# A gated MLP rewritten in two phases: up-projection by two levels of Strassen with weight sums made by accumulating DMAs, down-projection with resident weights

## What is computed

```python
hn = rmsnorm(x, norm1_g);  proj = hn @ w_in            # 1024 -> 3608
# ... both head groups, chunked; mix = concat(o_a, o_b)
x = x + mix @ w_out
hn2 = rmsnorm(x, norm2_g)
up, ffn_new = causal_dwconv(hn2 @ w_up, st_ffn, ffn_conv_w)   # 1024 -> 2*2816, float32
a_f, b_f = jnp.split(up, [D_FF], axis=-1)              # D_FF = 2816 = 22 * 128
x = x + (jax.nn.silu(a_f) * b_f) @ w_down              # 2816 -> 1024
y = rmsnorm(x, norm_f_g)
```

## Time and profile before

| | |
|---|---|
| median of 3 runs | 3259.01 us (3258.15 to 3260.91) |
| profiled execution, span from first to last instruction | 3255.5 us |
| mixers, to the first matmul of the MLP | 1600.7 us |
| MLP, from there to the end of the span | 1654.8 us |
| PE busy | 3173.5 us, 97% of the span |
| DVE busy | 2029.6 us, 62% |
| ACT, POOL busy | 26%, 18% |

### The profile page before, as it was taken

One profiled execution on the slowest core, in us unless ns is written; L12 is line 12 of the kernel. 1 busy time (PEld: TensorE's weight loads), 2 busy tenths in 40 slices (PEclk: granted clock), 3 DMA queues, 4 the chain that ended last, 5 costly groups with the idle time before them and its releaser, 6 DMA issues.

```text
span 3255.5 us, 56610 instructions
## 1 busy us (share of the span) xinstructions
PE 3173.5 (97%) x22353; PEld 2088.1 (64%) x22353; DVE 2029.6 (62%) x4672; ACT 833.7 (26%) x1743; POOL 580.7 (18%) x935
## 2 busy tenths in 40 slices
PE   7999999999999999997799999999999999999998
PEld 4555565566655565554577777777767767777765
DVE  2556666655566665655565666666676666666668
ACT  2222333223223333233321112111232211221213
POOL 1111111111111110112331211121053121111110
PEclk9999999999999999997899999999999999999999
DMA  7022222222222222215611111111133111111112
GB/s 242 27 67 85 85 77 75 85 67 69 66 75 85 85 66 85 80 52 159 205 50 39 52 52 39 39 52 39 39 124 119 48 43 52 39 39 39 47 31 78
DMA packets 223188, 236.37 MB, mean 73 GB/s; under 512 B 14204, under 2 KB 167332, under 8 KB 222931
## 3 DMA queue, kind: packets, MB, share of 16 engines
q1 hardware_dynamic: 222931, 232.81, 22.7%
HBM read 203.10 MB, written 29.67 MB: 72 GB/s over the span
## 4 chain that ended last, share of the span: by engine, by line
PE 50%; DVE 1%; issue 0%; ACT 0%; DVEq 0%
PE mlp_bank L2139 33%; PE mlp_bank L2213 15%; PE mlp_bank L2227 2%; PE mlp_bank L2219 0%; DVE mcv L2588 0%; DVE arena L2552 0%; DVE acc L2649 0%; DVE arena L2553 0%; PE mlp_bank L2238 0%; ACT raw L2331 0%; PE mlp_bank L2225 0%; DVE mcv L2592 0%; DVE arena L2560 0%; DVE arena L2557 0%; DVE raw L2520 0%
## 5 line engine op out<-in xcount | busy, mean ns | idle before, releaser
L710 PE MATMUL mixer_bank<-arena,hnt 128*128 128x451 f32 x2048 | 862.5, 552 | 9.2 <-DMA arena<-in_w_in_dram 8.4
L2139 PE MATMUL mlp_bank<-arena,ws 128*128 128x256 f32 (+1 forms) x2816 | 646.2, 383 | 3.8 <-DVE raw L2526 3.8
L2139 PEld LDWEIGHTS mlp_bank<-arena,ws 128*128 128x128 f32 x2816 | 535.7, 190 | 85.8 <-DVE raw L2526 4.6
L710 PEld LDWEIGHTS mixer_bank<-arena,hnt 128*128 128x128 f32 x2048 | 365.8, 190 | 298.0 <-issue 291.5
L2213 PE MATMUL mlp_bank<-arena 128*128 128x512 f32 x1120 | 493.8, 593 | 1.0 <-DVE arena L2560 1.0
L2621 DVE TENSOR_TENSOR acc<-acc,mlp_bank 128x512 f32<-128x512 f32 x560 | 370.8, 686 | 55.5 <-PE mlp_bank L2213 54.8
L2213 PEld LDWEIGHTS mlp_bank<-arena 128*128 128x128 f32 x1120 | 213.1, 190 | 235.2 <-issue 206.2
L647 POOL TENSOR_TENSOR ex<-dtt,level 128x512 f32<-128x512 f32 (+1 forms) x114 | 142.9, 1254 | 935.6 <-DVE dtt L1671 637.3
L2588 DVE SCALAR_TENSOR_TENSOR mcv<-raw,cf,mcv 128x512 f32<-128x512 f32 (+2 forms) x352 | 262.8, 762 | 50.3 <-ACT mcv L2302 41.5
L2139 PE MATMUL mlp_bank<-arena 128*128 128x256 f32 (+1 forms) x1056 | 250.1, 387 | 5.6 <-PEq L2731 4.6
L744 PE MATMUL mixer_bank<-wo,th 128*128 128x512 f32 x512 | 248.0, 607 | 2.9 <-DMA wo<-in_w_out_dram 2.2
(11 more groups left out here) (368 smaller groups left out, 3577.9 us busy)
## 6 DMA issues: line engine op xcount, KB each, us to landing
wo<-in_w_out_dram SPq DMA_DIRECT2D x260, 256.0 KB, 2.9
arena<-in_w_up_dram SPq DMA_DIRECT2D x44, 512.0 KB, 4.9
wu<-in_w_up_dram SPq DMA_DIRECT2D x44, 512.0 KB, 4.9
arena<-in_w_down_dram SPq DMA_DIRECT2D x40, 512.0 KB, 4.0
arena<-in_w_in_dram SPq DMA_DIRECT2D x7, 1804.0 KB, 16.0
xc<-in_x_t_dram SPq DMA_DIRECT2D x16, 512.0 KB, 4.3
xt<-in_x_prompt_dram SPq DMA_DIRECT2D x16, 512.0 KB, 5.0
xr<-in_x_prompt_dram SPq DMA_DIRECT2D x16, 512.0 KB, 3.6
```

What stands on the lines that cost most here:

```text
L710: x = pe.matmul(bank[ring(g)][0:N, 0:GW], hnt[:, k, 0:N], w[:, k, g * GW:(g + 1) * GW], start=(k == 0), stop=(k == KT - 1))
L2139: x = pe.matmul(out[:, 0:N], left[:, k, :], xb[:, slot, k, g * N:(g + 1) * N], start=first and k == 0, stop=k == HK - 1, skip_group_check= ...
```

## The change

The input projection, the heads and the output projection in `mixers` are as before. Changed are four things.

**1. Weights in blocks, and their sums in DRAM.** `w_up` is laid out by the host in 4 x 4 blocks (`w_blk`; reordering only). Two levels of Strassen need sums of blocks: S1 to S4 of the outer level (`s_blk`, 4 x 5.77 MB), and for each of the 7 outer operands four inner sums (`q_blk`, 4 x 10.1 MB). They are made in DRAM, beside the mixers: a plain copy from DRAM to DRAM, issued by ACT behind its work on a tile (12 copies, behind tiles 0 to 10 and 12), and one tile later an accumulating DMA onto it, issued by POOL behind its work on a tile (12 sums, two DMAs each). Copies and sums move 5.77 MB each, those of R1 to R4 4.3 MB. SP waits for all of them before it loads the first weight sums at the end of the mixers.

**2. Up-projection.** For each of the two passes 11 pairs of tiles f, each with 7 outer products n, each of 7 inner products of 2 matmuls (N = 256, 264). Two outer products are interleaved on PE. A ring of 7 holds weights (0.92 MB for each n, loaded afresh in both passes). ACT copies the running bank as before, DVE adds and subtracts the inner products, then adds whole outer products, 128x1024 (`outer`). The input sums of both levels, 32 instructions in each pass, are now DVE's (`x_sum`). The convolution is as before; its result goes to DRAM, `act_t`.

**3. Down-projection**, after all of 2. `w_down` and its sums lie in SBUF for good (11 pairs). For 8 groups q of 256 tokens and 11 pairs, 7 products with N = 512 each, summed over the pairs in PSUM; the last pair is done by Strassen too. DVE makes the activation sums (`unit_sums`) and takes each q out in 11 additions.

**4. The turn from 2 to 3.** The sums of pairs 0 and 1 of `w_down` and of the first activations are POOL's, placed behind its `keep` of the last pair; those of pairs 2 to 10 are DVE's, behind the last convolution.

```diff
+            def stash_copy(t):                                  # ACT, behind mixer(t)
+                for n, (at_, dst, src, sums) in enumerate(STASH_COPIES):
+                    if at_ == t:
+                        if n:
+                            act.wait_ge(s_stash_copied, 16 * n)
...
+                        act.dma_start(dst, src).then_inc(s_stash_copied, 16)
+            def stash_sum(t):                                   # POOL, behind mixer(t)
...
+                        half = dst.shape[0] // 32 * 16
+                        for r in (slice(0, half), slice(half, dst.shape[0])):
+                            gp.dma_start(dst[r], src[r], accum_op=ALU.add, max_dma_last_dim=8192)\
+                                .then_inc(s_stash_added, 16)
...
+            for d in range(DUOS):                               # PE, 77 duos
+                a, b = 2 * d, 2 * d + 1
+                product(a, 1)
+                product(b, 1)
+                product(a, 2)
+                product(b, 2)
+                product(a, 6)
+                product(b, 6)
+                if d:
+                    product(a - 2, 3)
+                product(a, 7)
+                product(b, 7)
+                product(a, 5)
+                product(b, 5)
+                product(a, 4)
+                product(b, 4)
+                if d:
+                    product(b - 2, 3)
...
+            load_sums(1)                                        # SP, start of the MLP
+            load_x(0, 2, 0, 0)
+            load_sums(2)
+            load_raw(3)
+            load_sums(3)
+            sp.dma_start(cwt, ffn_taps).then_inc(s_taps_in, 16)
+            load_x(0, 1, 0, 1)
+            load_x(0, 0, 1, 0)
...                                                             # stores of the states, 3 MB
             sp.wait_ge(s_states_out, 16 * (2 * H + 1))
...
+                keep(g, 0)                                      # POOL, each pair
+                keep(g, 1)
+                if g == NG - 1:
+                    w_sums(gp, 0, s_wt_gp, 0)
+                    unit_sums(gp, 0, s_us_gp, 0)
+                    w_sums(gp, 1, s_wt_gp, 4)
...
+                    x = pe.matmul(psum[:, acc_bank(q, k), :], left, right, start=(i == 0), stop=(i == PAIRS - 1),
+                                  skip_group_check=True)
```

More of the change, by code:

```diff
@@ new lines, in mlp @@
+        ua = [v[:, 0:1024].rearrange("p (f n) -> p f n", f=4) for v in U_AT]
+        us = [v[:, 1024:1792].rearrange("p (i f n) -> p i f n", i=3, f=2) for v in U_AT]
+        y = [room[:, 20304 + D * i:20304 + D * (i + 1)] for i in range(2)]
+        gf = room[:, 22352:23376]
+        first, chain = room[:, 23376:23888], room[:, 23888:24400]
+        junk = room[:, 24400:25424]
+        tailt = room[0:2 * FT, 24400:24400 + 18 * C].rearrange("p (r c) -> p r c", c=C)
+        sa = room[:, 25424:26128].rearrange("p (f n) -> p f n", f=FT)
@@ new lines, in block_of, with which_conv, tile_half, sampled @@
+        def block_of(n):
+            return 6 - n % 7
+        def which_conv(slot):
+            for k, off in enumerate((4, 7, 9, 10)):
+                g, rest = divmod(slot - off, 7)
+                if rest == 0 and 0 <= g < NG:
+                    return 4 * g + k
+            return None
+        def tile_half(c):
+            g, k = divmod(c, 4)
+            ps, i = divmod(g, PAIRS)
+            return ps, 2 * i + k // 2, k // 2, k % 2
+        def sampled(c):
+            return c // 4 >= PAIRS and c % 2 == 1
@@ L2134, in _ @@
+            sp.wait_ge(s_sample_out, 1)
+            sp.dma_start(y_s, y_sample.rearrange("p e n -> p (e n)")).then_inc(s_y_stored, 16)
+            store_y(Q - 1)
+            sp.wait_ge(s_y_stored, 16 * (2 * Q + 1))
         @block.tensor
         def _(pe):
-            def product(out, left, slot, ps, g, first):
-                N = PASSES[ps][2]
-                for k in range(HK):
-                    x = pe.matmul(out[:, 0:N], left[:, k, :], xb[:, slot, k, g * N:(g + 1) * N],
-                                  start=first and k == 0, stop=k == HK - 1,
-                                  skip_group_check=not first)
-                return x
@@ new lines, in first_taps @@
+            def first_taps(c):
+                ps, f, i, half = tile_half(c)
+                g, k = divmod(c, 4)
+                sample = sampled(c)
+                n = 2 * HALF_N[ps] - (S if sample else 0)
+                act.wait_ge(s_comb, made(g, k))
+                if half:
+                    act.wait_ge(s_edge, edge(g, ("pre12", "pre22")[i]))
+                    if sample:
+                        act.wait_ge(s_edge, edge(g, ("keep12", "keep22")[i]))
+                elif ps:
+                    act.wait_ge(s_edge, edge(g, ("outer0", "outer1")[i]))
+                else:
+                    act.wait_ge(s_zeros, 2)
+                if c == 0:
+                    act.wait_ge(s_taps_in, 16)
+                if c >= 2:
+                    act.wait_ge(s_act, c - 1)
+                for e in range(2):
+                    w0 = cwt[:, e * FT + f, 0:1]
+                    x = act.activation(cv[c % 2][:, e, 0:n], xo[i][:, half, e, 0:n], ACT.Identity, scale=w0)
+                    x.then_inc(s_first_tap, 1)
@@ L2489, in _ @@
[L2489 to L2509 removed]
+                    c = slice(e * FT + f, e * FT + f + 1)
@@ L2680, in finish_parts @@
-            def finish_parts(ks):
-                parts = [(partial(finish, 0, k, ORDER[k]),) for k in ks]
-                return [parts[2 * g:2 * g + 2] for g in range(len(parts) // 2)]
-            def pair(ps, i, p):
-                act_part, (first, second) = (partial(act_parts, ps, i - 1, 1 - p),), weight_parts(ps, i - 1)
-                last = up(ps, i, p, 0, (((), act_part), (first, second)))
-                if fixed(i, 2):
-                    dve.wait_ge(s_acc_ready, ps + 1)
-                down(ps, i - 1, 0)
-                last()
-                closing = fixed(i, PAIRS) and i == PAIRS - 1
-                last = up(ps, i, p, 1, combine_parts(ps) if closing else ())
-                down(ps, i - 1, 1)
-                last()
@@ new lines, in hook @@
+            def hook(d, at):
+                for ps, table in enumerate((HOOKS, LATER)):
+                    for name in table.get((d, at), ()):
+                        x_sum(ps, name)
+            for d in range(DUOS + 3):
+                a, b = 2 * d, 2 * d + 1
+                if which_conv(a - 1) is not None:
+                    silu_gate(which_conv(a - 1))
+                if which_conv(a) is not None:
+                    taps(which_conv(a))
+                hook(d, "A")
+                if 0 <= a - 2 < NP:
+                    subtract_q(a - 2)
+                    outer(a - 2)
+                if which_conv(a) is not None:
+                    silu_gate(which_conv(a))
+                hook(d, "B")
+                if a < NP:
+                    add_pq(a)
+                    add_pq(b)
+                hook(d, "C")
+                if which_conv(b) is not None:
+                    taps(which_conv(b))
+                if 0 <= b - 2 < NP:
+                    subtract_q(b - 2)
+                    outer(b - 2)
```

1601 lines of the change are left out of this document (859 added, 742 removed), and 6 rows, old and new, of the table X_ORDER.

## The result

The changed kernel takes **3477.31 us** (median of 4 runs, 3474.67 to 3480.44) against 3259.96 for the kernel before (4 runs): ratio **1.066**, 95% interval 1.065 to 1.068. It is slower by 217 us; the forecast was 3171.7, 88 us faster, with a range up to 3290. The sign is wrong and the time lies outside the range. The profiled execution has a span of 3474.4 us.

A forecast was written before the change was run, and what follows sets the result against it. PE, busy 97% of the time, was taken to bound the kernel. From 3259.0 us, the MLP's -113.3 and the mixers' +26 gave 3171.7 us, with a range from 3115 to 3290.

The forecast's parts named there:

- the mixers' unknown term: Mixers: PE waits 2.2 us for a load in each of 12 tiles, +26 us; bounds nothing and 223 us.
- Rival 1: Mixers: copies hold back `xc` and `wo`, PE waits 12 us in each of 12 tiles, +144, 3290 us; chance 0.19.
- POOL could be held: Mixers, end of a tile: POOL may be held for 25 us before PE needs its `ug`.
- The prices of PE: MLP matmuls: 0.432 us each with N = 256, 0.445 with N = 264, 0.858 with N = 512.
- rival 2: Up-projection: DVE becomes the bound, taking 5% longer than PE, 47 us, 3219 us; chance 0.15.
- Rival 3: Whole kernel: hardly any stall, copies free, passes without a gap, turn at its lower bound, 3119 us; chance 0.16.
- rival 4: PE doesn't run products of two matmuls back to back; no price of its own, counted with rival 2 (0.15).
- The MLP: Up- and down-projection with stalls and tail: 1541.5 us instead of 1654.8, -113 us.
- (a): Start of the MLP: PE waits for the first weights, 5 to 15 us, taken as 10.
- (b): Between the up-projection's passes: PE waits while DVE makes 32 input sums, 0 to 20 us, taken as 8.
- (c): Turn from up- to down-projection: PE waits 18 us for POOL's sums, plus 3 for a cold restart; bounds 10 and 28.
- The tail: After the last matmul: three additions instead of one and a full tile, 9.5 us instead of 7.3, +2 us.

The follow-up runs named there:

- copies alone: The changed kernel without the accumulating DMAs and the waits for them, the copies left where they are: 3350.11 us.
- The same with small packets: The kernel "Behind the residual's store" with its copies cut into 2 KB packets: 3313.21 us, ratio 1.017.
- Behind the residual's store: The changed kernel, with ACT's copy and POOL's second accumulating half issued only after the tile's residual rows are stored: 3210.91 us, ratio 0.9853.

## Why the prediction was wrong

**The step that failed is the mixers' unknown term: +26 us forecast, +304 measured.** It took a wait of PE in an ordinary crowd, 2.2 us, for each of 12 tiles. That row holds SP's own loads against each other, all of 0.5 to 2 KB a packet. It says nothing of a load beside a queue of 8 or 44 KB packets. What the runs showed in its place: `xc` and `wo` wait at the DMA engines for nearly as long as the copy and the second half of the accumulating DMA last, and PE for them, 268 us in all. The upper bound, a copy's own time of 19 us per tile, was exceeded too: about 25 us a tile (its 223 us also took 5.77 MB for all twelve copies; four carry 4.3 MB, which makes 205), since the second half of the accumulating DMA, which the bound left out, lies on the same spot. The condition was known, "the copy falls exactly on the output projection", and it was priced like an ordinary crowd.

**Rival 1 was what happened**, mechanism and place, with 0.19. Its price, 144 us, was half the loss. It turned the sign from 9.4 us a tile on, and with the copies alone the tiles with 5.77 MB already waited 13.4 us or more. The rule of the Trainium skill that stood beside it ("DMA: Bandwidth & Descriptors", section "Queues, rings and completion order": turns between queues, a packet at a time) agrees with the trace, if what the profile counts as a packet is the page's packet: 47 packets to 48 at 0.39 and 0.02 MB, and the tile with 2 KB packets bears it out. The chance should have followed the arithmetic of sizes: 0.5 KB against 8 or 44 KB leaves a load a few hundredths of the engines until the others are through, so the wait is nearly the others' whole time. The same page of the Trainium skill ("Latency and other measured facts") gives 214 GB/s for copies between HBM tensors; without the accumulating DMAs they were faster here, 5632 KB in 22.4 us, 257 GB/s (`s_blk<-in_w_blk_dram`, copies alone). Bytes and their time had been nearly right; who pays was not.

**What was right.** POOL could be held: its first DMA goes out at 825.13, the second at 840.71, `ug` is at 848.62 and had waited for DVE, and PE never waits for it. The prices of PE: 200 matmuls of pass 0 take 0.432 each, as forecast, and 196 of pass 1 take 0.4485, forecast 0.445; the down-projection's 148 take 0.860, forecast 0.858. Pieces of the chain of waits, to set beside the earlier trace rows:

```profile
2299.81 86.48 PE mlp_psum L2372 x400
...
2675.31 87.91 PE mlp_psum L2372 x392
...
3332.87 127.24 PE mlp_psum L2466 x296
```

DVE is not the bound (rival 2): 76% busy where PE has no gap, forecast 82, and no wait of PE for it recurs. A window of pass 0, against the earlier trace rows:

```profile
2000.00:2100.00 100.00, 100.00 (x465) 88.02 (x464) 75.81 (x115) 42.26 (x94) 3.46 (x10) 1.00 0.54 173
```

Rival 3 (hardly any stall) and rival 4 (no products back to back) fall by the same rows.

**The MLP: -85.5 us measured, -113 forecast.** The stalls are 54.6 us in the list of waits above, the forecast had 36 and some 6 for cold starts. (a) Start: 6.4 for DMA and 4.8 for PE's sequencer, forecast 10. (b) Between the passes: 9.3 + 7.2 + 2.8 for DVE's input sums, 19.3, forecast 8, at the upper end of 0 to 20; the slack in the banks took less of the 21 than I had given it. (c) Turn: 21.7 + 2.4, forecast 18. Around each the granted clock is lower, 0.92 on average from 1905 to 2000, 0.90 from 2400 to 2500, and 0.88 from 2900 to 3000.

The tail from the last matmul (3460.1) to the end is 14.3 us instead of 9.5: some ten additions follow it one after another, not three. Waits +19, tail +5 and some 4 us for the clock and the price of pass 1 make the 28 us that were missing. None of this changes the sign: with the mixers unharmed the kernel without transfers ran at 3172.01 us, so the MLP's part was worth 87 us, and the forecast's 3171.7 is near it by two errors that cancel, not by merit.

**What stays open.** In the three kernels that wait for the residual's store and keep the large packets, the mixers are still 35 to 47 us longer than before; they have the same mixers, so 11 us of this is scatter. In the best one it is 46.7, of which 26.7 us are PE's gaps without a releaser; the rest is not accounted for. That the gaps are late instruction fetches is argued from the times of the packets of q8; no kernel here changed the fetches alone. Open too is what 2 KB packets would give with all twelve copies on 16 engines; only four single tiles show it.

## What to carry to other kernels

Price a background transfer by its packets and its duration, not by the bandwidth that is left over: until it is through, a load of small rows that shares the engines gets one packet for each of its large ones, and whoever waits for that load waits nearly the transfer's whole time (here its time less some 7 us). So look in the trace for the stretch in which no engine waits for a load or a store, and issue the transfer there. Behind the output projection instead of ahead of it turned +6.6% into -1.4%. Waiting for the residual's store as well took away the wait that it was meant to take away, and no time that can be told from the scatter; with POOL's new order at the turn the best kernel is at -1.9%. Cutting the copy into packets of 2 KB helped the load beside it (5.8 us of waiting instead of 13.6 in one tile), but look how the cut copy runs: eight of twelve ran on 4 engines, and those who waited for their end paid more than was won. When a wait is removed, find the second latest operand first.

## What the runs showed of the hardware

- Queues share the DMA engines by packet, as counted: 48 packets of SP to 47 of POOL in 2 us, where SP's 0.5 KB packets had 6.0% of the engines beside POOL's 8 KB ones; 62 of SP to 61 of ACT in 10 us, where SP had 2.5% beside 44 KB packets.
- Between 8 and 44 KB the size of a copy's packets changed nothing for the load beside it (PE's wait 13.6 to 14.5 us against 13.4 to 14.1, behind 5632 KB); at 2 KB the wait fell from 13.6 to 5.8 us in the tile that can be compared.
- A copy within HBM of 5632 KB took 20.3 to 22.4 us in 8 or 44 KB packets, with no accumulating DMA beside it. Cut into 2 KB packets with a dimension of 4 outermost it took 73 us, at a share of the engines of 0.26 and 0.27 (windows from 900 and from 910 us of "The same with small packets"), and ended with 4 packets of 4 bytes instead of 16: by this reading on 4 of the 16 engines.
- POOL's second accumulating DMA, next in its list with nothing to wait for, was issued only 14.46 us after the first one's issue had ended, and POOL did nothing in between.
- PE can lose time to nothing that has a releaser: 23 to 30 us in 16 to 21 pieces in a stretch of many tiny matmuls, when copy and accumulating DMA wait for the residual's store; 7.2 to 7.6 us when they come right behind the output projection; 1.8 us where they stand in the changed kernel. In the kernel "Behind the residual's store" each piece ends 2.2 to 2.9 us after a packet of the instruction queue starts.
